# Modulation weights on their own queue and fp32 strips, eight gate rows, an earlier `mem`, and a reordered residual norm

## What is computed

```python
for l in range(DEPTH):                                   # first block, DEPTH = 2
    f = swiglu(rmsnorm(h, g[0]), w_ffn_gu[l, 0], w_ffn_down[l, 0])
    h = h + 0.5 * rmsnorm(f, g[1])
    z = rmsnorm(h, g[2]) @ w_in[l]
    zqk, zv, zo, zi, zf, zu, zsv, zxq, zg = split_cols(z)
    ...   # mLSTM (gates zi, zf: 4 + 4 columns), spatial gating, attention to rmsnorm(mem, g[6])
    y = merged @ w_out[l]
    h = h + rmsnorm(y, g[3])
    f = swiglu(rmsnorm(h, g[4]), w_ffn_gu[l, 1], w_ffn_down[l, 1])
    h = h + 0.5 * rmsnorm(f, g[5])
...
mod_l = silu(c) @ ada_w[li] + ada_b[li]                  # second block, 6 x 1024 columns a layer
mod_c = silu(c_ctx) @ ada_w[li] + ada_b[li]
```

## Time and profile before

| | us |
|---|---|
| median of 3 runs | 3651.64 (3648.01 to 3651.83) |
| span of the profiled execution | 3653.5 |
| PE busy | 3299.4 (90%) |
| DVE busy | 2006.5 (55%) |
| ACT busy | 1506.5 (41%) |
| POOL busy | 284.2 (8%) |

### The profile page before, as it was taken

One profiled execution on the slowest core, in us unless ns is written; L12 is line 12 of the kernel. 1 busy time (PEld: TensorE's weight loads), 2 busy tenths in 40 slices (PEclk: granted clock), 3 DMA queues, 4 the chain that ended last, 5 costly groups with the idle time before them and its releaser, 6 DMA issues.

```text
span 3653.5 us, 54212 instructions
## 1 busy us (share of the span) xinstructions
PE 3299.4 (90%) x22548; PEld 2827.8 (77%) x22548; DVE 2006.5 (55%) x2677; ACT 1506.5 (41%) x2136; POOL 284.2 (8%) x291
## 2 busy tenths in 40 slices
PE   7989999899898999989889688898899979996997
PEld 6978887797787888779767468887688868786795
DVE  4556645555555664555533666663433367676554
ACT  5445444445454555444532343332323244412443
POOL 1000000000000000000010224330000000023000
PEclk9999999999898999989989789998999989977999
DMA  7756545576675554557541000002232223500453
GB/s 223 225 161 178 151 150 180 161 228 199 192 226 155 167 163 152 178 158 230 179 126 52 0 2 8 2 3 81 66 98 92 92 65 91 145 1 5 138 179 133
DMA packets 461499, 459.75 MB, mean 126 GB/s; under 512 B 18272, under 2 KB 347168, under 8 KB 461280
## 3 DMA queue, kind: packets, MB, share of 16 engines
q1 hardware_dynamic: 454720, 435.42, 39.9%
q0 software_dynamic: 6560, 21.19, 1.9%
HBM read 455.50 MB, written 1.05 MB: 125 GB/s over the span
## 4 chain that ended last, share of the span: by engine, by line
PE 75%; DVE 15%; ACT 5%; issue 3%; DMA 1%; POOL 0%; DVEq 0%; ACTq 0%; SPq 0%; POOLq 0%
PE banks L305 20%; PE banks L307 19%; PE banks L306 19%; DVE weights_lo L291 1%; PE banks L1875 1%; PE banks L1874 1%; PE banks L4244 1%; PE banks L1300 1%; PE banks L3487 1%; PE banks L3489 1%; PE banks L3468 1%; DVE arena L3890 1%; PE banks L1897 1%; ACT weights_hi L283 1%; DVE arena L1433 1%
## 5 line engine op out<-in xcount | busy, mean ns | idle before, releaser
L291 DVE TENSOR_TENSOR weights_lo<-raw_weights,weights_hi 128x1024 fp32r<-128x1024 f32 (+1 forms) x463 | 548.6, 1191 | 500.9 <-ACT weights_hi L283 425.9
L283 ACT ACTIVATE weights_hi<-raw_weights 128x1024 fp32r<-128x1024 f32 (+1 forms) x463 | 474.0, 1031 | 624.5 <-PE banks L307 620.9
L256 DVE TENSOR_TENSOR weights_lo<-raw_weights,weights_hi 128x1024 fp32r<-128x1024 f32 x180 | 220.8, 1228 | 477.8 <-ACT weights_hi L249 288.9
L249 ACT ACTIVATE weights_hi<-raw_weights 128x1024 fp32r<-128x1024 f32 x180 | 190.4, 1060 | 521.6 <-PE banks L307 514.4
L305 PE MATMUL banks<-first_input_split,weights_hi 128*128 128x256 f32 x1320 | 379.6, 288 | 14.5 <-DVE weights_lo L291 7.8
L307 PE MATMUL banks<-first_input_split,weights_lo 128*128 128x256 f32 x1320 | 375.0, 284 | 0.0
L306 PE MATMUL banks<-first_input_split,weights_hi 128*128 128x256 f32 x1320 | 373.3, 283 | 0.0
L291 DVE TENSOR_TENSOR third_weights_split<-raw_weights,third_weights_split 128x1024 fp32r<-128x1024 f32 (+1 forms) x205 | 246.0, 1200 | 165.6 <-ACT third_weights_split L283 130.4
L283 ACT ACTIVATE third_weights_split<-raw_weights 128x1024 fp32r<-128x1024 f32 (+1 forms) x205 | 212.1, 1035 | 209.2 <-PE banks L307 207.4
L305 PE MATMUL banks<-work_split,weights_hi 128*128 128x512 f32 (+2 forms) x776 | 271.6, 350 | 22.9 <-DVEq L2374 19.1
L305 PEld LDWEIGHTS banks<-first_input_split,weights_hi 128*128 128x128 f32 x1320 | 251.5, 191 | 24.1 <-DVE weights_lo L291 10.6
(11 more groups left out here) (605 smaller groups left out, 7156.0 us busy)
## 6 DMA issues: line engine op xcount, KB each, us to landing
raw_weights<-in_w_ffn_gu SPq DMA_DIRECT2D x176, 512.0 KB, 4.9
raw_weights<-in_w_in SPq DMA_DIRECT2D x144, 512.0 KB, 3.6
raw_weights<-in_mlp_w SPq DMA_DIRECT2D x128, 512.0 KB, 3.9
raw_weights<-in_ada_w SPq DMA_DIRECT2D x96, 512.0 KB, 4.3
raw_weights<-in_w_ffn_down SPq DMA_DIRECT2D x80, 512.0 KB, 3.6
raw_weights<-in_w_branch SPq DMA_DIRECT2D x48, 512.0 KB, 3.5
raw_weights<-in_ssd_w_in SPq DMA_DIRECT2D x48, 512.0 KB, 3.9
raw_weights<-in_w_mkv SPq DMA_DIRECT2D x32, 512.0 KB, 3.9
```

What stands on the lines that cost most here:

```text
L249: last = s.activation(self.w_hi[:, u % 2, :], self.raw[:, u, :], ACT.Copy)
L256: last = v.tensor_tensor(self.w_lo[:, u % 2, :], self.raw[:, u, :], self.w_hi[:, u % 2, :].bitcast(F32), ALU.subtract)
L283: last = s.activation(hi, raw, ACT.Copy)
L291: last = v.tensor_tensor(lo, raw, hi.bitcast(F32), ALU.subtract)
```

## The change

1. **Modulations.** They leave the streams. `modulation_columns` itself loads each unit on POOL's queue into one of five slots (`MOD_SLOTS`) of the arena, and PE waits for it and multiplies it as it is, in plain fp32: four products of 256 columns, each with 32 stationary columns (two conditions and columns whose results nobody reads) into its own strip of 32 partitions of one bank. Nothing of it is split. The four strips are summed by the turn into columns, with `pick` as the other operand. The order is four modulation units in four half units of the stream, then four half units without.
2. **Gates.** The eight gate columns come as eight rows of 256 tokens (24 products of 256 columns for 48 of 8), and two small transposes (L1375 of the changed kernel) turn them.
3. **Start and memory.** x comes in two DMAs, one for each half; a root is taken ahead of it; `mem` is loaded right behind the parameters in layer 0, and in both layers the chain first lets eight half units pass. `condition` is written behind the parameters' wait.
4. **Transitions.** `add_normed` multiplies the product rows of the second tile by scale and weight while ACT squares those of the first, and the other way round; the root comes in the residual's sum.

```diff
 def add_normed(c, done, gain, scale):
+    def gained(t, semaphore, value):
+        @c.block.vector
+        def _(v):
+            gain.wait(v)
+            v.wait_ge(semaphore, value)
+            v.scalar_tensor_tensor(two_halves(c.y[:, t, :]), product_rows(c, t), scale, two_halves(gain.buf),
+                                   ALU.mult, ALU.mult).then_inc(c.rows_gained, 1)
...
+    first, second = c.tile
+    try_root(c)
+    second_gained = gained(1, c.multiplied, done)
+    first_squared = squared(0, first, c.multiplied, done)
+    root_of_mean(c, first, c.ss[:, 0, 0:1])
+    squared(1, second, *second_gained)
+    root_of_mean(c, second, c.ss[:, 1, 0:1])
+    gained(0, *first_squared)
     for t, ch in enumerate(c.tile):
         reciprocal_of(c, ch, c.ss[:, t, 0:1])
 
         @c.block.vector
         def _(v):
-            gain.wait(v)
-            v.wait_ge(ch.steps_done, ch.steps)
-            v.scalar_tensor_tensor(two_halves(c.y[:, t, :]), product_rows(c, t), c.ss[:, t, 0:1],
-                                   two_halves(gain.buf), ALU.mult, ALU.mult).then_inc(ch.steps_done, 1)
-        ch.steps += 1
-        @c.block.vector
-        def _(v):
-            v.wait_ge(ch.steps_done, ch.steps)
-            v.scalar_tensor_tensor(c.h[:, t, :], c.y[:, t, :], scale, c.h[:, t, :], ALU.mult,
+            v.wait_ge(c.rows_gained, c.gained)
+            v.wait_ge(ch.steps_done, ch.steps)
+            v.scalar_tensor_tensor(c.h[:, t, :], c.y[:, t, :], c.ss[:, t, 0:1], c.h[:, t, :], ALU.mult,
                                    ALU.add).then_inc(ch.steps_done, 1)
...
+    def bring_modulation_weights(m, free=()):
+        u, n = m % UNITS, m // UNITS
+        src = token_units(a["ada_w_2"][n // 12], n % 12 * BANK)[u][0]
+        @c.block.gpsimd
+        def _(g):
+            for semaphore, value in free:
+                g.wait_ge(semaphore, value)
+            if m >= MOD_SLOTS:
+                g.wait_ge(c.mods_multiplied, m - MOD_SLOTS + 1)
+            g.dma_start(mod_slots[m % MOD_SLOTS], src).then_inc(c.mods_arrived[m % MOD_SLOTS], 16)
...
+                    pe.wait_ge(c.mods_arrived[m % MOD_SLOTS], 16 * (m // MOD_SLOTS + 1))
+                    if u == 0:
+                        pe.wait_ge(c.mods_taken, rows_free)
+                    for j in range(2):
+                        k = 2 * u + j
+                        for half in range(2):
+                            strip = (2 * j + half) * STRIP
+                            last = pe.matmul(c.ps[strip:strip + STRIP, 6, 0:SEQ], c.conditions[:, 2 * k:2 * k + STRIP],
+                                             slot[:, j, half * SEQ:(half + 1) * SEQ], start=(u == 0),
+                                             stop=(u == UNITS - 1))
+                    last.then_inc(c.mods_multiplied, 1)
...
+        def eight_times(pe, banks, u, part, hi, lo):
+            k = 2 * u + part
+            return c.three_products(pe, c.ps[0:8, banks, 0:SEQ], hi[:, part, :], lo[:, part, :], x_in[0][:, k, :],
+                                    x_in[1][:, k, :], k == 0, k == KD - 1)
...
-        out = [Stretch(token_units(w_in, 3 * D, 8), tokens_times(c, x_in, 8), eight, ready=input_made)]
+        out = [Stretch(token_units(w_in, 3 * D, 8), eight_times, eight, ready=input_made)]
...
+    bring_memory()
     stream = feed_forward_streams(0, 0)
-    normed_input(c, slots[0], x_in, stream)
-    conditions_made = condition()
-
-    @c.block.tensor
-    def _(pe):
-        pe.wait_ge(*conditions_made)
+    try_root(c)
+    normed_input(c, slots[0], x_in, stream, c.x_arrived)
...
         @block.sync
         def _(sp):
-            sp.dma_start(c.h[:, :, :], a["x"].rearrange("o (t p) d -> p (o t) d", p=P)).then_inc(x_arrived, 16)
+            for t in range(NT):
+                sp.dma_start(c.h[:, t, :], a["x"][0, t * P:(t + 1) * P, :]).then_inc(c.x_arrived[t], 16)
```

195 lines of the change are left out of this document (94 added, 101 removed).

## The result

The changed kernel takes 3618.25 us (median of 4 runs, 3615.51 to 3624.13) against 3651.73 for the kernel before: a ratio of 0.9907, 95% interval 0.9894 to 0.992. That is 33.5 us less, where 41.4 were forecast. The profiled execution of the changed kernel has a span of 3615.5 us, 38.0 less than that of before. 6.3 of these 38.0 lie in the second block, which the change doesn't touch; TensorE stood at half clock there for 324 us before and for 301 us after.

The account below looks back on a forecast made before the run. PE was taken as the bound, dense in the feed-forwards, carrying 75% of what ended last. Terms summed to 60.4 us gained and 19 lost, 41.4 less than the median of 3651.6: 3610 us, range 3590 to 3638.

Parts of the forecast that it names:

- the clock behind `mem`: Half clock going with the removed `mem` waits: 1.4 us gained at the start, 3.4 in layer 1.
- The unit on PE: Each of 96 modulation units falls from 0.93 to 0.70 us on PE, four strips side by side: 22 us gained.
- the sign of being right: From a modulation unit's first strip to the next 256-column product lie 0.65 to 0.75 us.
- The turns into columns: 24 turns of modulation chunks, with 128 stationary rows instead of 4, save 0.17 us each: 4 us gained.
- Cover lost: Modulations finish earlier, so PE's wait for DVE before the down projection grows 0.93 us, four times: 4 us lost.
- Arrival: PE waits for the first modulation weights of each of four series; with half clock 15 us lost, between 5 and 25.
- Transitions: One DVE pass leaves the chain behind the root at six norm transitions, 1.3 us each: 8 us gained (5 to 9).
- Start and layer 1's memory: Earlier first product and no `mem` waits, with half clock: 8 us gained at the start, 7.4 in layer 1.
- Gates: 24 products of 256 columns replace 48 of 8: 5.5 us gained a layer, between 1.6 and 8.6; 11 for two.
- Rival 1: DMA engines become the bound in modulation series, limited to 262 GB/s: 17 us back, 3627 us; chance 0.14.
- rival 2: Strips run in pairs, a modulation unit takes 1.07 or 1.1 us: 38 us back, 3648, no change; chance 0.07.
- Rival 3: Strips run one behind the other, unit 1.9 us: 3725; slower once a unit costs over some 1.3 us; chance 0.06.

Follow-up runs that it names:

- late_fours: The changed kernel with each modulation series begun eight half units later and a chunk's four units back to back; 3577.4 us, 0.9793 of the kernel before.
- two_strips: The changed kernel with a modulation unit's four products in two strips, two after each other in each; 3666.4 us, 1.0034 of the kernel before.
- late: The changed kernel with each modulation series begun eight half units later, its loads issued where they were; 3603.6 us, 0.9866 of the kernel before.
- mem_back: The changed kernel with `mem` and its chain where they were before, modulation units unmoved; 3620.4 us, 0.9901 of the kernel before.
- gates_back: The changed kernel with the eight gate columns as before (48 products of 8 columns, no transposes); 3635.1 us, 0.9935 of the kernel before.

## Why the prediction came out as it did

It was right in direction, and the time lies in its range, 8 us above the forecast. Part of the nearness is luck: the terms that were too small (turns, transitions and gates, 4 us together) offset a part of those too large (the units by 6 us, the clock behind `mem` by up to 10). By its own steps:

- **The unit on PE** is the step that was mis-sized: 22 us counted, 96 x 0.165 = 16 measured. The mechanism was right. The price was taken from L2877 in the earlier trace rows as the time from its first row to the next group's start, "with the change of shape on either side". But between those two starts the unit took 0.57 us and not 0.70, outside the 0.65 to 0.75 that were named as the sign of being right; and 0.19 more, which the forecast put at nothing, lie outside them: 0.09 in the step ahead of the group, and 0.10 between the first and the second product behind it. The row that shows the latter (65.01 in the trace of before) stood next to the earlier trace rows and wasn't read. Of late_fours' 0.33 us for a change of shape the forecast had 0.27 (0.70 less two rounds of 0.216). The rule of the Trainium skill that was weighed (TensorE: Matmul & The Clock Gate, Part 3), with its gain of 18 us, came nearer to the 16. It came nearer by another way, though: it has the strips lose some of their overlap, and two_strips shows that here they lose none. Nor does the trace agree that a stationary load overlaps a product only where the row group differs: all strips use the same 128 rows, and in late_fours the second round's stationary loads run from 82.06 to 82.18 us beneath the first round's products (82.03 to 82.43).
- **The turns into columns**: 4 counted, 0.276 x 24 = 6.6 measured. Against both edges of the old form only one is left. That makes 22.4 for units and turns together, against 26.
- **Cover lost**: 4 counted; the four waits went from 3.5 us in all to 7.3, 3.8. Right.
- **Arrival**: 2.4, 5.4 and 4.5 us were worked out, with clock 15. Measured were 2.9, 5.3, 1.7 and 3.0, 12.8 in all, and 16 with half clock, by late. Right, each at the place named, though the loads took 5.7 to 7.0 us to land and not 5.3.
- **Transitions**: 1.3 us each, 8 counted; 1.45 to 1.65, 8.9 measured, by the waits in the traces.
- **Start and layer 1's memory**: the first product came 1.2 us earlier, as counted. The waits of 5.6, 4.0 and 0.8 us are gone; one of 0.67 us for `conditions` came (at 47.84). But the sum took them, and arrival's waits, as two terms. mem_back shows that they are one: with `mem` late, the first feed-forwards' arrival waits vanish, and only 3 us lie between the two kernels. Since arrival had been costed from the changed order, the sum itself was not wrong for it; a reader who asks what the early `mem` is worth would be, by 10 us. What was oversized is its clock: 4.8 us had been credited to less half clock, and the feed-forwards had more of it (47 against 37 us), which costs up to 5.
- **Gates**: 5.5 a layer counted, between 1.6 and 8.6. 5.5 and 6.4 measured, 6.9 and 5.8 by gates_back. The size was right, by neither of the two ways that bounded it: the clock did fall, but ahead of the products, in the transition's wait, and it rose again before or as they ended. Half clock in mixing went from 34 to 21 us, which is up to 6.6 of the 11.8.
- **Rival 1**, that the DMA engines bound the series: no unit inside a series waits. 262 GB/s, from the earlier trace rows, was no ceiling. A window of the changed kernel behind the burst of loads shows more, the share there being full, and more for each tenth of the share (372 GB/s at 1.04 against 206 at 0.70), as the prediction's reason against this rival would have it, though what makes it so wasn't separated:

```profile
55.12:58.53 3.41, 3.41 (x20) 2.37 (x19) 0.00 (x0) 0.00 (x0) 0.79 (x2) 0.50 1.04 372
```

- **Rivals 2 and 3**, strips in pairs or in series: two_strips is what rival 2's kernel would be, 1.0034 with 6.7 us for its slower turns in it. The forecast of "no change" for it was close. Rival 3's kernel was not run; in this one the four strips' starts, 7 ns apart, exclude it. Its turning point was miscounted: 37.5 doesn't follow from the sum, by which the change breaks even at 0.93 + (41.4 - 22)/96, 1.13 us a unit, and not at 1.3. two_strips, whose unit costs 1.18 with its edges, lies beyond, and was slower.

Added up, with the measured sizes: 15.8 + 6.6 + 8.9 + 1.2 + 10.4 + 11.8 gained, 3.8 + 12.8 and up to 5 of half clock lost, 33 to 38 us; the medians differ by 33.5. The profiled spans differ by 38.0, by the second block's 6.3 and against 1.3 lost in the output projections, where half clock fell otherwise. What makes half clock fall in one run's output projection and not in another's was not tried.

## What to carry to other kernels

A change of shape on TensorE has to be read over three steps: ahead of the group, in it, and one product behind it. Here that was 0.33 us, more than two fifths of a small unit, so small odd-shaped products belong in one bunch and not strewn between others: that gave 22 us without removing any work. A prefetch ring that is filled in one burst takes its bandwidth from whatever streams at that time. Fill it early, and one load at a time, behind the consumer's own progress. And when a wait is taken away ahead of a queue's entry, ask what stood behind that entry: here five loads.

## What had not been expected

- Strips: a round of two and a round of four 32-column strips both take 0.216 us, with starts 6 to 7 ns apart.
- The 128-row, 2-column plain fp32 products enter from fp32r products without a cost (0.12 us), while four-row ones and column strips pay 0.09 us; behind all three the step is 0.20 to 0.23. With 64 rows (two_strips) the entry costs 0.09 too. So for plain fp32 the entry's cost goes with the shape, and the cost behind does not. Shape alone isn't it: before, the fp32r products of four stationary columns paid neither (0.11 us ahead of the group, 0.12 behind). What makes the cost behind wasn't separated: a strip product in fp32r was not run.
- Five 512 KB loads on POOL's queue together with the stream's on SP's ran the DMA engines at a share of 1.02 for 10.9 us. Three loads of the stream issued from 47.6 to 50.0 took 13.2 to 14.4 us to land. The Trainium skill (DMA: Bandwidth & Descriptors, Queues, rings and completion order) says that each DMA engine takes turns between the queues that it has work for; the trace agrees, in that both moved bytes while the burst lasted, 3032 KB on POOL's queue and 894 on SP's between 48.0 and 60.5 us. What sets these shares was not tried.

The median load on POOL's queue took longer than in the earlier trace rows:

```profile
arena<-in_ada_w POOLq DMA_DIRECT2D x96, 512.0 KB, 6.7
```
